# 1/rms spread, token combinations, one bank and GpSimd's split reordered in a two-block FFN kernel

## The reference

```python
def rmsnorm(x, g):
    y = x32 * lax.rsqrt(jnp.mean(x32 * x32, axis=-1, keepdims=True) + EPS)
    return y.astype(x.dtype) * g

def swiglu(h, w_in, w_out):
    gate, up = jnp.split(h @ w_in, 2, axis=-1)
    return (jax.nn.silu(gate) * up) @ w_out

x = x + 0.5 * swiglu(rmsnorm(x, ffn_norm), w_in, w_out)    # D 1024, D_FF 2816
```

## Time and profile before

| | before |
|---|---|
| median of 3 runs | 1722.51 us |
| profiled execution | 1723.04 us |
| its span | 1721.3 us |
| mean granted clock of TensorE | 0.998 |
| TensorE matmul busy | 1693.5 us, 98% |
| VectorE busy | 954.4 us, 55% |
| ScalarE busy | 736.5 us, 43% |
| GpSimd busy | 769.7 us, 45% |

### The profile page before, as it was taken

How to read it: one execution, slowest core, us unless ns; L and a number is a source line. 1 busy time by engine, 2 the same in 40 slices (tenths; PEclk the granted TensorE clock), 3 DMA queues, 4 the chain that set the end, 5 groups by cost and what they waited for, 6 DMA issues and landing times.

```text
span 1721.3 us, 25382 instructions
## 1 busy us (share of the span) xinstructions
PE 1693.5 (98%) x9725; PEld 1447.8 (84%) x9725; DVE 954.4 (55%) x1277; ACT 736.5 (43%) x1027; POOL 769.7 (45%) x366
## 2 busy tenths in 40 slices
PE   7999999999999999999999999999999999999998
PEld 5677788777788899998889888888888889999887
DVE  5645765655766787776320634641113587777412
ACT  4445773644573544445333322332222444445323
POOL 1342635242225545554444444444444445555552
PEclk9999999999999999999999999999999999999999
DMA  9614215112113223222333322222222222332222
GB/s 364 236 56 165 74 50 220 63 60 98 50 50 109 90 99 118 97 90 85 101 100 114 107 91 96 98 98 94 93 92 87 98 98 98 106 114 75 92 93 83
DMA packets 35062, 180.88 MB, mean 105 GB/s; under 512 B 4487, under 2 KB 6669, under 8 KB 19373
## 3 DMA queue, kind: packets, MB, share of 16 engines
q1 hardware_dynamic: 30876, 166.09, 27.0%
q10 hardware_dynamic: 4112, 13.80, 2.2%
HBM read 177.78 MB, written 2.10 MB: 104 GB/s over the span
## 4 chain that ended last, share of the span: by engine, by line
PE 83%; DVE 6%; issue 5%; POOL 3%; ACT 1%; SPq 1%; DMA 1%; POOLq 0%; DVEq 0%; ACTq 0%
PE ps L1352 20%; PE ps L1354 20%; PE ps L1353 20%; PE ps L1650 3%; PE ps L1652 3%; PE ps L1651 3%; POOL wl_both L659 3%; PE ps L1414 1%; PE ps L1419 1%; PE ps L1415 1%; PE ps L1717 1%; PE ps L1691 1%; DVE fl L2645 1%; SPq L566 1%; DMA ada_w<-w_ada 1%
## 5 line engine op out<-in xcount | busy, mean ns | idle before, releaser
L659 POOL TENSOR_TENSOR wl_both<-raw_both,wh_both 128x1024 fp32r<-128x1024 f32 (+1 forms) x184 | 424.0, 2325 | 501.5 <-ACT wh_both L793 497.4
L1352 PE MATMUL ps<-xh,wh_both 128*128 128x512 f32 (+1 forms) x880 | 315.4, 358 | 1.2 <-POOL wl_both L681 1.2
L1354 PE MATMUL ps<-xh,wl_both 128*128 128x512 f32 (+1 forms) x880 | 312.1, 355 | 0.0
L1353 PE MATMUL ps<-xl,wh_both 128*128 128x512 f32 (+1 forms) x880 | 312.1, 355 | 0.0
L793 ACT ACTIVATE wh_both<-raw_both 128x2048 fp32r<-128x2048 f32 x91 | 174.2, 1914 | 318.0 <-PE ps L1354 308.1
L681 POOL TENSOR_TENSOR wl_both<-raw_both,wh_both 128x1024 fp32r<-128x1024 f32 x46 | 114.2, 2498 | 206.8 <-ACT wh_both L947 137.9
L1352 PEld LDWEIGHTS ps<-xh,wh_both 128*128 128x128 f32 x880 | 166.4, 189 | 31.7 <-issue 7.9
L1354 PEld LDWEIGHTS ps<-xh,wl_both 128*128 128x128 f32 x880 | 166.4, 189 | 23.4
L1353 PEld LDWEIGHTS ps<-xl,wh_both 128*128 128x128 f32 x880 | 166.5, 189 | 22.1
L702 POOL TENSOR_TENSOR wl_both<-raw_both,wh_both 128x1024 fp32r<-128x1024 f32 x72 | 148.8, 2089 | 19.4 <-ACT wh_both L1145 19.4
L1352 PE MATMUL ps<-fh,wh_both 128*128 128x512 f32 (+1 forms) x374 | 141.4, 378 | 1.6 <-POOL wl_both L659 1.5
(11 more groups left out here) (361 smaller groups left out, 3998.9 us busy)
## 6 DMA issues: line engine op xcount, KB each, us to landing
raw_both<-ffn_in_stream SPq DMA_DIRECT2D x44, 1024.0 KB, 4.8
raw_both<-mixer_stream SPq DMA_DIRECT2D x40, 1024.0 KB, 4.8
raw_both<-layer_stream SPq DMA_DIRECT2D x36, 1024.0 KB, 5.6
raw_both<-ffn_out_stream SPq DMA_DIRECT2D x32, 704.0 KB, 4.0
ada_w<-w_ada SPq DMA_DIRECT2D x16, 512.0 KB, 11.4
ada_late<-w_ada ACTq DMA_DIRECT2D x16, 512.0 KB, 5.0
gate_w<-w_ada ACTq DMA_DIRECT2D x4, 1024.0 KB, 12.9
next_w<-w_ada SPq DMA_DIRECT2D x7, 512.0 KB, 9.1
```

The source lines that it names most:

```text
L659: last = nc.gpsimd.tensor_tensor(wl[u][:, cols], raw[u][:, cols], wh[u][:, cols].bitcast(F32), ALU.subtract)
L1352: nc.tensor.matmul(bank_ap, w0, x0, start=first, stop=False, skip_group_check=goes_on)
L1353: nc.tensor.matmul(bank_ap, w0, x1, start=False, stop=False, skip_group_check=goes_on)
L1354: return nc.tensor.matmul(bank_ap, w1, x0, start=False, stop=last, skip_group_check=goes_on)
```

## The change

Four places are edited, in both FFNs.

1. `norm_spread` moves from behind chunk 0 to between its seventh and its eighth k-step.
2. The token combinations are made in the order t3, t1, t2, t4 instead of t1, t2, t4, t3. The two that read only SBUF come first, back to back. ScalarE's silu of the second late gate moves behind the high parts of t3 and t1.
3. `keep_u2` moves from behind the fourth weight sum of the next chunk to between the second and the third.
4. GpSimd waits before `split_three` of a chunk until its weight sums are made. In the tail the split of the second output chunk goes before the last product, and `fl` is made in groups of 1, 2, 3, 4 in place of 2, 2, 2, 4.

```diff
--- before.py
+++ after.py
@@ -695,9 +695,10 @@
                     nc.gpsimd.tensor_tensor(total[:], next_at[next_place(n_)][:], total[:], ALU.add
                                             ).then_inc(next_added, 1)
 
-            def split_three(i, c, plain, u):
+            def split_three(i, c, plain, u, ffn_):
 
                 pool.wait_ge(w_high, i * 2 + (plain + c + u + 1))
+                pool.wait_ge(s_sums, i * 6 + 3 * (ffn_ * SEVEN + c - STD + u + 1))
                 for cols, done in ((slice(0, 2 * QC), half_split), (slice(2 * QC, 3 * QC), w_ready)):
                     nc.gpsimd.tensor_tensor(wl[u][:, cols], raw[u][:, cols], wh[u][:, cols].bitcast(F32),
                                             ALU.subtract).then_inc(done, 1)
@@ -723,20 +724,20 @@
                         split(size, 0, chunk, plain + c - c % 2, c % 2)
                         if c >= 2:
                             late_product(name, c - 2)
-                    split_three(0, STD, plain, 0)
-                    split_three(0, STD, plain, 1)
+                    split_three(0, STD, plain, 0, n // 5)
+                    split_three(0, STD, plain, 1, n // 5)
                     product(0, name, STD, 0)
                     with pool.Fori(0, (SEVEN - 2) // 2) as i:
-                        split_three(i, STD + 2, plain, 0)
+                        split_three(i, STD + 2, plain, 0, n // 5)
                         product(i, name, STD, 1)
-                        split_three(i, STD + 2, plain, 1)
+                        split_three(i, STD + 2, plain, 1, n // 5)
                         product(i, name, STD + 2, 0)
                     plain += count
                     continue
                 if n in (3, 6):
                     split(size, 0, chunk, plain, 0)
+                    split(size, 0, chunk, plain, 1)
                     product(0, "ffn1" if n == 3 else "ffn2", FT - 2, 1)
-                    split(size, 0, chunk, plain, 1)
                     with pool.Fori(1, count // 2) as i:
                         for u in range(2):
                             split(size, i, chunk, plain, u)
@@ -1186,11 +1187,12 @@
                     if k == 1:
                         gate_late(0)
                 take_high(chunk + 3)
-                gate_late(1)
-                for n_, (halves, bank) in enumerate(((t1, 4), (t2, 6), (t4, 4), (t3, 6))):
-                    act.wait_ge(tmp_ready, SPLIT0[f"tok{ffn_ + 1}"] + (2, 3, 3, 4)[n_])
+                for n_, (halves, bank) in enumerate(((t3, 6), (t1, 4), (t2, 6), (t4, 4))):
+                    act.wait_ge(tmp_ready, SPLIT0[f"tok{ffn_ + 1}"] + (2, 2, 4, 4)[n_])
                     nc.scalar.activation(halves[0].rearrange("p (b a) c -> p b (a c)", b=2), ps[:, bank:bank + 2],
                                          ACT.Copy).then_inc(high_ready, 1)
+                    if n_ == 1:
+                        gate_late(1)
                 blocks_high(0, STD, 0)
                 gate_std(2)
                 sums_high(0, STD, 0)
@@ -1427,6 +1429,10 @@
                 first_steps(moving, low0, range(KT - 2))
                 if sums_of is not None:
                     norm_sums(sums_of)
+                    first_steps(moving, low0, range(KT - 2, KT - 1))
+                    norm_spread(sums_of)
+                    first_steps(moving, low0, range(KT - 1, KT))
+                    return
                 first_steps(moving, low0, range(KT - 2, KT))
 
             def first_token_unit(unit, chunk, u, low0=None, sums_of=None):
@@ -1918,7 +1924,6 @@
                 unit, chunk = UNIT0[name], CHUNK0[name]
                 ffn_ = 0 if name == "ffn1" else 1
                 first_feature_unit(unit, chunk, (xh, xl), SPLIT0[f"norm{n}"], n)
-                norm_spread(n)
                 claim(0, unit, 1)
                 chunk_ready(0, chunk, 1)
                 for k in range(KT):
@@ -2569,7 +2574,7 @@
 
                     return ps[:, bank:bank + 2].rearrange("p b (a c) -> p (b a) c", c=HALF)
 
-                def sums(i, c, u, first=False):
+                def sums(i, c, u, first=False, between=()):
 
                     n_ = ffn_ * SEVEN + c - STD + u
                     if first:
@@ -2580,6 +2585,8 @@
                     dve.wait_ge(raw_landed[u], i * 16 + (16 * ((chunk + c) // 2) + 16))
                     nc.vector.tensor_tensor(ps[:, 4], a21, a22, ALU.add).then_inc(s_sums, 1)
                     nc.vector.tensor_tensor(ps[:, 6], a11, a21, ALU.subtract)
+                    if between:
+                        keep_u2(*between)
                     dve.wait_ge(s_sums, i * 6 + (3 * n_ + 1))
                     nc.vector.tensor_tensor(ps[:, 5], ps[:, 4], a11, ALU.subtract).then_inc(s_sums, 1)
                     dve.wait_ge(s_sums, i * 6 + (3 * n_ + 2))
@@ -2655,19 +2662,19 @@
                     low_x(k)
                 dve.wait_ge(tmp_ready, rewritten + KT)
                 nc.vector.tensor_tensor(t_bank(4), quarter(1, 1), quarter(1, 0), ALU.subtract).then_inc(tmp_ready, 1)
+                nc.vector.tensor_tensor(t_bank(6), quarter(0, 1), quarter(1, 1), ALU.subtract).then_inc(tmp_ready, 1)
                 gate_late(1)
-                dve.wait_ge(tmp_ready, tok0 + 1)
+                low_t(0, t3, 6)
+                up_late(1)
+                dve.wait_ge(high_ready, tok0 + 2)
+                dve.wait_ge(low_ready, tok0 + 1)
                 nc.vector.tensor_tensor(t_bank(6), quarter(0, 1), t_bank(4), ALU.subtract).then_inc(tmp_ready, 1)
-                up_late(1)
-                low_t(0, t1, 4)
-                dve.wait_ge(tmp_ready, tok0 + 2)
-                dve.wait_ge(low_ready, tok0 + 1)
+                low_t(1, t1, 4)
+                dve.wait_ge(tmp_ready, tok0 + 3)
+                dve.wait_ge(low_ready, tok0 + 2)
                 nc.vector.tensor_tensor(t_bank(4), quarter(0, 0), t_bank(6), ALU.subtract).then_inc(tmp_ready, 1)
-                low_t(1, t2, 6)
-                dve.wait_ge(low_ready, tok0 + 2)
-                nc.vector.tensor_tensor(t_bank(6), quarter(0, 1), quarter(1, 1), ALU.subtract).then_inc(tmp_ready, 1)
-                low_t(2, t4, 4)
-                low_t(3, t3, 6)
+                low_t(2, t2, 6)
+                low_t(3, t4, 4)
                 sums(0, STD, 0, first=True)
                 up_std(2)
                 first_low(0, STD, 0)
@@ -2679,8 +2686,7 @@
                     nxt = (c, 1) if u == 0 else (c + 2, 0)
                     if not first:
                         up_first(i, *((c, 0) if u else (c - 2, 1)))
-                    sums(i, *nxt)
-                    keep_u2(i, c, u, first)
+                    sums(i, *nxt, between=(i, c, u, first))
                     first_low(i, *nxt)
                     keep_m15(i, c, u)
                     other_lows(i, *nxt)
@@ -2695,11 +2701,11 @@
                 seven(0, FT - 2, 0)
                 up_first(0, FT - 2, 0)
                 keep_u2(0, FT - 2, 1)
-                f_lows(range(0, 2))
+                f_lows(range(0, 1))
                 keep_m15(0, FT - 2, 1)
-                f_lows(range(2, 4))
+                f_lows(range(1, 3))
                 up_second(0, FT - 2, 1)
-                f_lows(range(4, 6))
+                f_lows(range(3, 6))
                 gate_second(0, FT - 2, 1)
                 f_lows(range(6, 10))
                 up_first(0, FT - 2, 1)
```

## The result

The changed kernel takes **1729.33 us**, median of six runs (1729.27 to 1730.27), against 1722.51 for the kernel before: ratio 1.004, with a 95% interval of 1.0027 to 1.0053. It is slower by 6.8 us.

The account below looks back on a forecast made before the run. TensorE was taken as the bound, busy without break in the loops, with some 8 us to win at the heads. Terms -2.8 - 2.2 - 1.8 + 17.9 = +11.1 on median 1722.51 gave 1733.6 us, range 1722 to 1741 (own 1728 to 1739).

Parts of the forecast that it names:

- The loop: Units 1 to 16 of both FFNs: moved kept_u makes TensorE wait for act_u, 0.56 us per unit, +17.9 us.
- The slack: Loop chain from fourth sum through act_u to the seventh block: 0.14 us per unit to spare.
- the shift of the third sum: In the loop, third sum comes 0.60 us later: 0.26 waiting for TensorE plus 0.34 of kept_u's issue.
- The heads: Unit 0 of each FFN gets shorter: -2.8 us in ffn1, -2.2 us in ffn2.
- the collision of the second combination with GpSimd's split: At the head, GpSimd takes over before the second token combination, which ends at about 587.4 instead of 585.1.
- The rival inside the forecast: At the head, VectorE keeps the port: gains 3.7 and 3.1 us, total 1731.8; chance 0.75 together with the forecast.
- the three collisions: At the head, sums held up by GpSimd's split; removal takes 2.2 us off unit 0's sums, 2.6 off unit 1's.
- rival D: In the loop, waits pull the clock grant down, 1.5 us each; at 8 of 32 units +12, about 1746; chance 0.05.
- 1/rms: Spread inside the first chunk: xs starts 0.8 us earlier, xl is done 0.45 us earlier.
- The tail: Ends of both FFNs: shorter waits for act_u and second output weights, third output chunk becomes the limit, -1.8 us.
- B: The loop hides the shift, period stays 10.08 us, only head and tail gains remain: about 1715 us; chance 0.12.
- C: In the loop, shift is only 0.34 us of issue and no restart is lost: about 1722 us; chance 0.08.

Follow-up runs that it names:

- e1: Kernel before with only kept_u moved between the second and third weight sum: 1737.89 us, ratio 1.0086.
- e2: Changed kernel with kept_u back behind the fourth weight sum, all other parts kept: 1714.21 us, ratio 0.9948.
- e3: e2 without GpSimd's wait for the weight sums: 1722.74 us, ratio 0.9999.
- e9: Kernel before with only GpSimd's wait for the weight sums added: 1714.84 us, ratio 0.9952.
- e4: e2 with 1/rms spread behind chunk 0 again, as in the kernel before: 1713.52 us, ratio 0.9945.
- e10: e2 with the first two token combinations each made as two instructions of 512 columns: 1713.35 us, ratio 0.9944.
- e6: e2 with the token combinations and ScalarE's silu in the order of before: 1713.28 us, ratio 0.9944.
- e8: e2 with ScalarE rounding the third output weight chunk ahead of the last four pieces of fh: 1712.08 us, ratio 0.9938.
- e5: Changed kernel with kept_u one place later, between the third and fourth weight sum: 1717.98 us, ratio 0.9969.

## Why the prediction was right, and where it was off

The forecast was 1733.6 us, slower, in a range of 1722 to 1741. The measured 1729.33 us lies in it, and near the lower end of the narrower 1728 to 1739, and the mechanism is the one foretold: a wait for act_u in every unit of the loop outweighs what heads and tails win. Point by point:

- **The loop, +17.9 foretold, +14.9 measured.** The chain was right: e1 alone gives it, e2 takes it away. The slack (0.14 foretold, 0.61 - 0.48 = 0.13 measured) and the restart (0.10) were right. The term that was mis-sized is the shift of the third sum: 0.60 us foretold, 0.50 measured in 14 of 16 units. Block 2's last matmul starts 2.76 us behind the unit's first and ends 0.28 later, and VectorE's kept_u follows it after 0.04 us (3.08 behind the unit's first). The forecast took this start from unit 17, where it is 3.18 us, 0.14 behind the matmul's end. Units 1 and 16 of after, which like unit 17 are written out in VectorE's list, show 3.18 too; here unit 1, whose first matmul is at 613.07:

```profile
616.25 0.42 DVE L2615 TENSOR_TENSOR kept_u<-ps,kept_m 128x256 f32<-128x256 f32 x1 [0.17 <-PE ps L1356]
```

These units take the foretold 10.64 us (10.62 to 10.64), those in the loop 10.53. So the 0.10 us goes with whether the unit's code is in a loop, on VectorE and ScalarE alike; what in that makes the difference isn't shown.
- **The heads, -2.8 and -2.2 foretold, -3.7 and -3.1 measured.** The step that failed is the collision of the second combination with GpSimd's split. The rival inside the forecast, that VectorE keeps the port, gave -3.7 and -3.1 and came out to the digit. The removal of the three collisions and of the clock's dip was right: e3 brings them back, and e9 alone removes them. Without the dip less is won than the 1.5 us that it takes: in the kernel before, the matmuls from 611.84 to 615.23 start 0.21 us apart in place of 0.12 and lose that much, but ffn2's unit 0, at full clock, loses 0.9 us to a wait for act_u that ffn1's doesn't have, and is only 0.58 us shorter. The forecast's two head gains, 0.6 us apart, have this right; rival D, at 1.5 us for each dip, left it out. In after GpSimd asked 0.24 us before the second combination, in e4 0.88 us, and it stood both times. The Trainium skill (SBUF — State Buffer, "Who interferes with whom") states that the order of issue decides who blocks; taken as the order of these starts, the traces don't bear it out here. Between two weight sums GpSimd does get in: in the kernel before it asked at 595.93, 0.45 us ahead of the second sum's start, and that sum stood, and so in e3 (598.50). What tells these cases apart is open; e10 shows that it isn't the instruction's length.
- **1/rms.** xs was to start 0.8 us earlier; it starts 0.75 earlier (570.47 against 571.22). xl ends 0.6 us earlier, foretold 0.45. To the time it is worth nothing (e4), as is the token order (e6): unit 0's sums start at 595.55 instead of 595.77, and what matters behind them is their length.
- **The tail, -1.8 foretold, -1.76 measured.** The steps came as foretold: at block 7 the idle time is 0.04 us instead of 0.64 (0.25 foretold), the second output weights are in time, and the third chunk is the next limit. It had 1.0 us to spare and not enough; e8 removes that limit and gives 1.2 to 1.4 us more.
- **The sum.** The loop's loss was put 3.0 us too high, the heads' gain 1.8 us too low: +11.1 foretold, +6.3 in the spans. Both errors pushed the forecast up, by 4.8 us together.
- **The rivals.** B (the loop hides the shift) and C (only 0.34 us of issue) were ruled out by 34 waits and 0.46 us per unit. C would have been nearer for the other place of kept_u: in e5 part of the issue is hidden behind the wait for the third sum, and 0.15 us per unit is left (period 10.23). D (the clock) didn't show: the granted clock is 1.00 in both loops of after, though each unit has a pause.
- **A row misread.** That a sum with one SBUF operand isn't held up was read from the third sum at 670.10, but GpSimd's product had ended at 669.63. The head shows it, where the split ran until 600.42:

```profile
595.93 4.49 POOL L702 TENSOR_TENSOR wl_both<-raw_both,wh_both 128x1024 fp32r<-128x1024 f32 x2 [5.61 <-ACT wh_both L1145]
599.19 0.69 DVE L2584 TENSOR_TENSOR ps<-ps,raw_both 128x512 f32<-128x512 f32 x1
```

## What to carry to other kernels

Before an instruction is moved forward in the queue of an engine with half its time idle, follow the chain that leaves the instructions it passes: if its slack is shorter than the issue of the moved one (0.13 us against 0.34 here), each turn of the loop pays, and 32 small stalls outweigh two large ones. Test the parts one by one: here one added wait, which keeps GpSimd off VectorE's operands, held 8 us of gain in itself, two parts were worth nothing beside it, and one cost 15 us. When a stall is removed, look at once for the transfer or split that was ready just behind it (the third output chunk, worth 1.2 us or more).

## What the runs showed of the hardware

- A GpSimd instruction that has already asked may stand behind two VectorE instructions with two SBUF operands in a row (0.24 us ahead of the second in after, 0.88 us in e4, ahead of the last two of four in e10), but gets in between two weight sums (the second sum lasts 2.89 us before and 1.78 in e3, in place of 0.70).
- After a semaphore wait TensorE's first spacing is longer than its pace: 0.22 us against 0.12 with 256 columns, 0.31 (807.83 to 808.14 in after) against 0.23 with 512. A stall of 0.05 us thus costs 0.15 (e5).
- The granted clock fell behind the long waits of ffn1's head (0.93 over 602 to 625 us in e3, as before), and stayed at 1.00 with the same waits at ffn2's head, with 0.6, 1.3 and 0.7 us in e1's heads, and with 34 short waits in after.
